# A two-block model's fp32 kernel: order of small stages in the mixer, and a shorter loop for overflowing experts

## The chip, the cores and the metric

One core of one Trainium2 chip runs the whole program in one launch. The metric is the device time of an execution in microseconds (us), the median over runs. PE stands for TensorE, DVE for VectorE, ACT for ScalarE, POOL for GpSimd, SP for SyncE.

## The reference

A sequence of 256 tokens of width 1024 passes two models' blocks, all in float32. The first block has a mixer (a gated delta rule with four heads in both directions over a context and the sequence, beside a Fourier mix) and a gated convolutional network. Norms are modulated by vectors made of a conditioning vector. The second block has two layers, each with a mixer, a layer of 32 experts of which each token uses two, and a gated embedding.

```python
mod_l = (silu_c @ w_ada[i] + b_ada[i])[:, None, :]                 # six rows of 1024: shifts, scales, gates
p = h @ w_in_l                                                     # u | q, k, v | z | a, b
qkv = silu(dwconv1d(p[..., o1:o2], conv_l)); q, k = l2norm(q), l2norm(k)
beta = sigmoid(ab[:, :, 0:2])
g = -exp(a_log) * softplus(ab[:, :, 2:4] + dt_bias)                # log decay
a_mat = where(strict, (kb @ kc.T) * decay, 0)                      # per chunk and head
t_inv = triangular_solve(eye + a_mat, eye)                         # then the scan over chunks
y_f = einsum(real(fft2(u)), w_f); y_d = rmsnorm(o) * silu(z)
y = concatenate([y_f, y_d]) @ w_out
...
h = h + hier_moe(rmsnorm(h), ...)                                  # silu(x @ w_gate[e]) * (x @ w_up[e]) @ w_down[e]
gate = sigmoid(rmsnorm(h) @ w_ple_gate + b); h = h + gate * (p @ w_ple)
```

## The kernel before

Activations stand transposed, features on the 128 partitions and tokens along the free axis. Each engine has a program written out by hand, in one order, and engines meet by counting semaphores. Dense weights come in chunks of 128 x 4096 floats (2 MB) into a ring of tiles in SBUF (`ring`), in the order of the table `DENSE`; SP issues the loads one after another (L420), each behind a wait for the products that used the slot's last content. `plan()` works these waits out.

Large projections use three rounded products in place of one fp32 product: ACT rounds a chunk half by half (`split_half`, L1232), and POOL (L1683) or DVE (`weights_low`, L1796) subtracts it from the chunk, which leaves the remainder. PE's `split_product` (L527) waits for the remainder of each half. All other products are fp32 (`dense`, L520), and PE carries out each fp32 product as two matmul instructions with two weight loads, and each transpose as one with one.

Results of `dense` and of the projections go through four PSUM banks in turn. `USES` numbers these uses in PE's order; use n takes bank n modulo 4, may start when use n - 4 is released, and counts up the semaphore `dense_full` when done. So `USES` is an order that PE, ACT, DVE and the load plan share.

The first block's mixer goes as follows. The projection w_in has five chunks: k and v (two), q, z, u. DVE does the short convolutions (L1900 to L1903), ACT the silu. The gates' logarithm is a chain of small DVE instructions (`log1p`, L1840 to L1848). For the l2 norms of six head tiles (four of k, two of q) DVE squares (L1934), PE sums over partitions (`sums_qk`, L671), ACT takes the root as a logarithm and an exponential (`root`, L1212 and L1213), DVE multiplies (L1950). In between ACT copies finished banks out (`to_sbuf`, L1325). After the Fourier weight products dft_w come the sums of the decay rates (L713) and, through `heads` (L704), the products of keys with keys and the rows of decay and beta; DVE takes differences (L1969), POOL masks (L1704), ACT exponentiates, DVE makes the key matrices (L1982), eight in number, counted by `at_ready`. DVE then inverts all 32 by 32 diagonal blocks in 31 steps of two instructions (L2020, L2022), with the column copies of the modulation (`ada_columns`, L2012) after steps 7, 12, 17 and 22, while PE transposes v and k (L696), and does the Fourier products (dft_b, dft_y) and parts 1 and 2 of the modulation. A part is four row products (L625, each with a chunk of its own), each followed by a copy of the row out of its bank, and four column products that turn the row into columns (through L520). Then the triangular solve goes on in larger blocks (L788 onward), which waits for DVE's solve and for all uses of part 2, and ACT copies diagonal blocks behind its last row copy.

The expert layers run in hardware loops over pairs of experts, four pairs to a turn on PE (L1084). Each expert has 64 slots; tokens beyond them go through an overflow loop over all experts under a branch on a flag (L1093 on PE, others on SP, ACT and DVE). Behind the branch PE starts the projection of the embedding's gate, whose first matmul (L527) needs the first of eight remainders that DVE makes (`weighted_low`, L1786); DVE multiplies the bank of that projection at L2340.

## Time and profile before

| what | value |
|---|---|
| median of 3 runs | 1750.52 us (1749.62 to 1752.70) |
| the profiled execution | 1751.42 us |
| its span, first to last instruction | 1749.6 us |
| mean granted TensorE clock | 0.973 |
| PE / DVE / ACT / POOL busy | 94% / 41% / 29% / 13% |
| moved by DMA | 528.27 MB, mean 302 GB/s |

The span is what all times in rows are counted from; the execution's own time is 1.8 us longer. A busy PE is not PE at its peak, since the ends of matmuls are modelled. The granted clock is a share of full speed (2.4 GHz); 0.50 is the lower level, 1.2 GHz. "issue" means that the engine waited for nothing that the profile shows.

### The profile page before, as it was taken

The page shows a single profiled execution, that of the slowest core. Times are in us where ns is not written, and L with a number is a line of the kernel's source. Part 1 is how long each engine was busy: PE and PEld are TensorE (multiplying, and loading weights), DVE is VectorE, ACT ScalarE, POOL GpSimd, SP SyncE. Part 2 cuts the span into 40 slices and gives each one's busy share as a digit, 9 for nine tenths or more (in the row PEclk, how much of TensorE's full clock was granted, in tenths as well). Part 3 has the DMA queues.
Part 4 walks back from the last instruction along what each step waited for, and adds up shares of the span by engine and source line. Part 5 has one row for each costly group of instructions (what it writes and reads, how often), then busy time and mean ns, then how long its engine had stood idle before and what let it go on. Part 6 is the DMA issues. An engine that isn't in the chain of part 4 may idle for free.

```text
span 1749.6 us, 25579 instructions
## 1 busy us (share of the span) xinstructions
PE 1642.2 (94%) x10590; PEld 1119.9 (64%) x10590; DVE 722.9 (41%) x1348; ACT 506.8 (29%) x778; POOL 231.7 (13%) x151
## 2 busy tenths in 40 slices
PE   5989898999999999999999997998999999999997
PEld 2778597899989964554435453988645454445446
DVE  2565724899346631222212124679322121212134
ACT  3344335544444221111111114476211110111125
POOL 0406313488420000000000000000000000000000
PEclk9999979999999999999999999999999999999998
DMA  9213516244454679999999999225899999999990
GB/s 403 106 38 129 241 60 242 105 184 148 166 193 186 272 309 420 428 427 429 428 429 428 428 427 406 103 92 217 369 420 428 427 430 427 429 428 428 426 396 25
DMA packets 37958, 528.27 MB, mean 302 GB/s; under 512 B 4208, under 2 KB 4336, under 8 KB 5104
## 3 DMA queue, kind: packets, MB, share of 16 engines
q1 hardware_dynamic: 37296, 525.22, 72.3%
q10 hardware_dynamic: 576, 1.78, 0.3%
q8 instruction: 68, 1.11, 0.2%
q14 instruction: 18, 0.15, 0.0%
HBM read 525.94 MB, written 1.05 MB: 301 GB/s over the span
## 4 chain that ended last, share of the span: by engine, by line
PE 69%; DMA 18%; DVE 8%; ACT 3%; issue 1%; POOL 1%; SPq 0%; DVEq 0%; ACTq 0%
PE bank L527 22%; PE bank L1050 18%; DMA ring<-in_w_up 10%; PE bank L1080 9%; PE bank L995 5%; DMA ring<-in_dense 4%; DMA work<-in_w_up 4%; PE bank L520 2%; DVE ring_rounded L1796 2%; PE bank L1016 1%; PE bank L1017 1%; ACT ring_rounded L1232 1%; PE bank L599 1%; PE bank L704 1%; PE bank L1065 1%
## 5 line engine op out<-in xcount | busy, mean ns | idle before, releaser
L527 PE MATMUL bank<-work_rounded,ring_rounded 128*128 128x256 f32 (+1 forms) x2192 | 358.2, 294 | 20.4 <-DVE xn_rounded L1786 7.1
L1050 PE MATMUL bank<-ring,work 128*64 128x512 f32 x1536 | 339.3, 596 | 17.7 <-DMA ring<-in_w_up 15.5
L527 PEld LDWEIGHTS bank<-work_rounded,ring_rounded 128*128 128x128 f32 x2192 | 310.3, 193 | 30.4 <-issue 16.3
L527 PE MATMUL bank<-xn_rounded,ring_rounded 128*128 128x256 f32 (+1 forms) x1536 | 276.3, 292 | 3.9 <-DVE xn_rounded L1780 3.4
L1050 PEld LDWEIGHTS bank<-ring,work 128*64 128x64 f32 x1536 | 114.1, 138 | 235.0 <-issue 221.9
L527 PEld LDWEIGHTS bank<-xn_rounded,ring_rounded 128*128 128x128 f32 x1536 | 224.5, 196 | 8.4 <-issue 4.4
L2286 DVE TENSOR_TENSOR work<-work,bank 128x512 f32<-128x512 f32 x32 | 22.0, 688 | 420.1 <-PE bank L1050 420.1
L1683 POOL TENSOR_TENSOR ring_rounded<-ring,ring_rounded 128x2048 fp32r<-128x2048 f32 (+1 forms) x37 | 159.5, 4329 | 209.9 <-ACT ring_rounded L1232 209.9
L1749 POOL TENSOR_TENSOR work<-work_rounded,work 128x128 f32<-128x128 f32 x64 | 24.2, 399 | 1139.3 <-PE bank L1073 825.8
L1080 PE MATMUL bank<-ring,work 128*64 128x512 f32 x768 | 170.1, 596 | 0.0
L1232 ACT ACTIVATE ring_rounded<-ring 128x2048 fp32r<-128x2048 f32 (+1 forms) x84 | 147.6, 1802 | 51.4 <-DMA ring<-in_dense 26.2
L995 PEld LDWEIGHTS bank<-work_rounded,work 128*128 128x128 f32 x1024 | 117.7, 193 | 24.7 <-issue 24.3
L1796 DVE TENSOR_TENSOR ring_rounded<-ring,ring_rounded 128x2048 fp32r<-128x2048 f32 (+1 forms) x47 | 102.4, 2203 | 58.3 <-ACT ring_rounded L1232 58.1
L995 PE MATMUL bank<-work_rounded,work 128*128 128x128 f32 x1024 | 123.2, 279 | 0.0
L2297 DVE SCALAR_TENSOR_TENSOR xn_rounded<-bank,work,work_rounded 128x512 fp32r<-128x512 f32 x64 | 48.0, 750 | 177.3 <-ACT work_rounded L1549 177.3
L1050 PE MATMUL bank<-work 128*64 128x512 f32 x512 | 112.8, 593 | 5.8 <-DMA work<-in_w_up 5.8
L1080 PEld LDWEIGHTS bank<-ring,work 128*64 128x64 f32 x768 | 53.0, 137 | 99.9 <-issue 99.9
L1539 ACT ACTIVATE work<-bank 128x512 f32<-128x512 f32 x30 | 18.0, 599 | 323.6 <-PE bank L995 323.6
L1549 ACT ACTIVATE work_rounded<-bank,work 128x512 fp32r<-128x512 f32 x64 | 44.0, 687 | 178.5 <-PE bank L1080 178.3
L2271 DVE TENSOR_TENSOR hT<-hT,bank 128x512 f32<-128x512 f32 x136 | 84.9, 682 | 8.9 <-PE bank L1017 8.9
L1050 PEld LDWEIGHTS bank<-work 128*64 128x64 f32 x512 | 38.1, 137 | 78.4 <-issue 78.4
L2104 DVE SCALAR_TENSOR_TENSOR work<-bank,params,work 128x189 f32<-128x189 f32 (+2 forms) x176 | 76.1, 432 | 6.2
(333 smaller groups left out, 1702.9 us busy)
## 6 DMA issues: line engine op xcount, KB each, us to landing
ring<-in_dense SPq DMA_DIRECT2D x48, 2048.0 KB, 7.9
ring<-in_w_gate SPq DMA_DIRECT2D x48, 2048.0 KB, 21.8
ring<-in_w_up SPq DMA_DIRECT2D x48, 2048.0 KB, 24.7
ring<-in_w_down SPq DMA_DIRECT2D x48, 2048.0 KB, 27.0
work<-in_w_gate SPq DMA_DIRECT2D x16, 2048.0 KB, 23.2
work<-in_w_up SPq DMA_DIRECT2D x16, 2048.0 KB, 25.6
work<-in_w_down SPq DMA_DIRECT2D x16, 2048.0 KB, 27.0
ring<-in_dense SPq DMA_DIRECT2D x8, 1408.0 KB, 6.2
```

Of the source, the lines that this page charges most:

```text
L520: last = mm(bank[n % BANKS][:, a:b], w, x, start=k == 0, stop=k == len(products) - 1)
L527: last = mm(out, rv(high_store[r][:, at:at + P]), rv(x[part][k]), start=opens and k == 0 and j == 0, stop=closes and k == n_k - 1 and j == 2)
L995: last = mm(out, xtok[:, u, k], rv(oneh[:, u].rearrange("p x s -> p (x s)")).bitcast(F32), start=u == 0, stop=u == NH - 1)
L1050: ins = mm(b[64 * y:64 * y + 64, :], xg[:, k, 64 * y:64 * y + 64], ws[y][:, 512 * k:512 * k + 512], start=k == 0, stop=k == KT - 1)
L1080: ins = mm(bank[6 + half][64 * y:64 * y + 64, :], hidT[:, j, 64 * y:64 * y + 64], ws[y][:, at:at + 512], start=j == 0, stop=j == 3)
L1232: signal(act.activation(rv(high_store[HIGH_SLOT[n]][:, a:b]), w[:, a:b], ACT.Copy), "w_high")
L1549: act.activation(rv(y_high[half]), bank[6 + half][:], ACT.Identity, scale=slot_w).then_inc(S["y_high"], 1)
L1683: pool.tensor_tensor(rv(w), w, rv(high_store[HIGH_SLOT[n]][:, a:b]), ALU.subtract).then_inc(S["w_low"], 1)
L1796: v.tensor_tensor(rv(w), w, rv(high_store[HIGH_SLOT[n]][:, a:b]), ALU.subtract).then_inc(S["w_low_dve"], 1)
L2104: ins = v.scalar_tensor_tensor(dst, x[:, r0 + dy:r1 + dy, c0 + dx:c1 + dx], par("w_dwc", 9 * f + 3 * (dy + 1) + dx + 1, 1), dst, ALU.mult, ...
L2271: v.tensor_tensor(hT[:, pair], hT[:, pair], bank[(5, 2, 3, 5)[q]][:].rearrange("p (k t) -> p k t", k=2), ALU.add)\
L2297: ins = v.scalar_tensor_tensor(rv(y_low[half]), bank[6 + half][:].rearrange("p (k t) -> p k t", k=2), slot_w, rv(y_high[half]).rearrange(" ...
```

## The change

It does five things. The overflow loop's body on PE becomes one for a half of the tokens, run 64 times, with wide products and transposes back in place of 32 narrow ones; DVE copies the half into a tile first, and copies the result out before the transposes. The remainders of chunk 3 of w_in (z) come ahead of the query convolutions on DVE, with ACT's rounding moved ahead too; chunk 4's (u) are put among the norms. On ACT the roots come ahead of the copies of z. On PE two groups of key products come ahead of the sums of the rates. And parts 1 and 2 of the modulation are spread: rows 0 and 1 of part 1 come between the token-major transposes and the Fourier products dft_b, row 0 of part 2 ahead of dft_y, with `USES` renumbered and a second buffer for rows (`ada_row`). Renamings through `ada_use` elsewhere are left out here.

```diff
@@ -85,10 +85,16 @@
 N_DENSE = sum(count for _, count, _ in DENSE)
 SPLIT = ("w_in", "w_out", "w_up", "w_down", "w_in_a", "w_out_a", "ple0", "w_in_b", "w_in_y", "w_out_b", "ple1")
-USES = [("ada0", 8), ("kv", 8), ("q", 2), ("z", 2), ("u", 2), ("dft_w", 2), ("vtok", 4), ("ktok", 4), ("dft_b", 4),
-        ("ada1", 8), ("dft_y", 2), ("ada2", 8),
+USES = [("ada0", 8), ("kv", 8), ("q", 2), ("z", 2), ("u", 2), ("dft_w", 2), ("vtok", 4), ("ktok", 4), ("ada1", 3), ("dft_b", 4),
+        ("ada1b", 5), ("ada2", 1), ("dft_y", 2), ("ada2b", 7),
         ("w_out", 4), ("up", FT), ("down", 4), ("in_a", 12), ("out_a", 4), ("ple0", 4), ("in_b", 4), ("gates0", 8), ("in_y0", 2), ("gates1", 8), ("in_y1", 2),
         ("out_b", 4), ("ple1", 4)]
+
+def ada_use(use, part, i):
+    first = (8, 3, 1)[part]
+    return use[f"ada{part}"] + i if i < first else use[f"ada{part}b"] + i - first
...
@@ -104,10 +110,10 @@
         use[name] = at
         at += count
     free = {}
-    for stage in ("ada0", "ada1", "ada2"):
+    for part in range(3):
         for c in range(4):
-            free[first[stage] + c] = ("dense_full", use[stage] + max(1, 2 * c))
+            free[first[f"ada{part}"] + c] = ("dense_full", ada_use(use, part, max(0, 2 * c - 1)) + 1)
     for c, last in enumerate((4, 8, 10, 12, 14)):
         free[first["w_in"] + c] = ("dense_full", use["kv"] + last)
...
@@ -309,7 +315,8 @@
     sqk = wk("cat", 1024).rearrange("p (n t) -> p n t", n=2)
     sqo = wk("kc", 1024).rearrange("p (n t) -> p n t", n=2)
     o_rstd = wk("kc", 1024, 1024).rearrange("p (n t) -> p n t", n=2)
-    ada_row = wk("cat", 1024, 1024).rearrange("p (m n) -> p m n", m=2)
+    ada_row = [wk("cat", 1024, at).rearrange("p (m n) -> p m n", m=2) for at in (1024, 0, 1024)]
     c_cols = wk("S", KT * 32).rearrange("p (k m) -> p k m", k=KT)
     ab_rows = wk("S", 512, 512)
...
@@ -704,14 +710,10 @@
                 last = mm(out[:, P * h:P * h + P], left(h), right(h), start=start, stop=stop)
             return last
-        for n in (USE["u"], USE["u"] + 1, USE["dft_w"], USE["dft_w"] + 1):
+        for n in (USE["u"], USE["u"] + 1):
             released(pe, n)
         pe.wait_ge(S["gates_ready"], 1)
         pe.wait_ge(S["qk_norm"], 6)
-        rates = glog.rearrange("p u c -> p (u c)")
-        for i, m in enumerate((cums[0], cums[1], ones)):
-            last = mm(bank[7][:, 32 * i:32 * i + 32], m, rates, start=True, stop=True)
-        signal(last, "gc_mm")
         def key_products(u, b):
...
@@ -734,8 +736,14 @@
             signal(heads(b, lambda h: beta[:, u, h:h + 1].to_broadcast([P, P]), lambda h: ident), "b_rows")
         key_products(0, 4)
+        key_products(1, 5)
+        for n in (USE["dft_w"], USE["dft_w"] + 1):
+            released(pe, n)
+        rates = glog.rearrange("p u c -> p (u c)")
+        for i, m in enumerate((cums[0], cums[1], ones)):
+            last = mm(bank[7][:, 32 * i:32 * i + 32], m, rates, start=True, stop=True)
+        signal(last, "gc_mm")
         decay_rows(0)
-        key_products(1, 5)
         for e in (1, 2, 3):
             decay_rows(e)
...
@@ -759,20 +767,23 @@
         token_major("vtok", vc)
         token_major("ktok", kc)
+        for m in range(2):
+            ada_step(1, m)
         for x in range(2):
             for u in range(NH):
                 dense(USE["dft_b"] + 2 * x + u, [
                     (P * g, P * g + P, [(uT[:, g, P * u:P * u + P], fo_w[:, x, P * g:P * g + P])]) for g in range(4)])
-        for m in range(5):
+        for m in range(2, 5):
             ada_step(1, m)
+        ada_step(2, 0)
         for b in range(4):
             released(pe, USE["dft_b"] + b)
         for b in range(2):
             dense(USE["dft_y"] + b, [
                 (SEQ * i, SEQ * i + SEQ, [(fo_b[:, x, u, 2 * b + i], fo(("cos_l", "sin_l")[x], SEQ * u, SEQ))
                                           for x in range(2) for u in range(NH)]) for i in range(2)])
-        for m in range(5):
+        for m in range(1, 5):
             ada_step(2, m)
...
@@ -781,6 +792,8 @@
         pe.wait_ge(S["solved"], 2)
         pe.wait_ge(S["att_ready"], 4)
+        for b in range(2):
+            released(pe, USE["dft_y"] + b)
         for s in range(2):
             for pair in range(2):
...
@@ -1091,27 +1104,31 @@
             over = pe.value_load(flag[0:1, 0:1], min_val=0, max_val=1)
             with pe.If(over > 0):
-                with pe.Fori(0, E) as e:
-                    pe.wait_ge(S[f"ov_full{layer}"], e * 48 + 48)
-                    for u in range(NH):
-
-                        pe.wait_ge(S[f"ov_add{layer}"], e * 2 + u + 1)
-                        for b in range(2):
-                            for k in range(KT):
-                                last = mm(bank[b][:], xnT[:, k, P * u:P * u + P], ring[2 * b + 1][:, 512 * k:512 * k + 512],
-                                          start=k == 0, stop=k == KT - 1)
-                        last.then_inc(S[f"ov_gu{layer}"], 1)
-                        pe.wait_ge(S[f"ov_hh{layer}"], e * 2 + u + 1)
+                with pe.Fori(0, NH * E) as n:
+                    pe.wait_ge(S[f"ov_add{layer}"], n * 2 + 1)
+                    for b in range(2):
+                        for k in range(KT):
+                            last = mm(bank[b][:], xg[:, k], ring[2 * b + 1][:, 512 * k:512 * k + 512],
+                                      start=k == 0, stop=k == KT - 1)
+                    last.then_inc(S[f"ov_gu{layer}"], 1)
+                    pe.wait_ge(S[f"ov_hh{layer}"], n * 2 + 1)
+                    for j in range(4):
+                        last = nc.tensor.transpose(bank[4][:, P * j:P * j + P], hh[:, P * j:P * j + P], ident)
+                    last.then_inc(S[f"ov_t{layer}"], 1)
+                    pe.wait_ge(S[f"ov_ht{layer}"], n + 1)
+                    for half in range(2):
                         for j in range(4):
-                            last = nc.tensor.transpose(bank[4][:, P * j:P * j + P], hh[:, P * j:P * j + P], ident)
-                        last.then_inc(S[f"ov_t{layer}"], 1)
-                        pe.wait_ge(S[f"ov_ht{layer}"], e * 2 + u + 1)
-                        for f in range(KT):
-                            out = bank[6 + f // 4][:, P * (f % 4):P * (f % 4) + P]
-                            for j in range(4):
-                                last = mm(out, ring[5][:, D * j + P * f:D * j + P * f + P], hidT[:, j],
-                                          start=j == 0, stop=j == 3)
-                        last.then_inc(S[f"ov_down{layer}"], 1)
+                            last = mm(bank[6 + half][:], hidT[:, j], ring[5][:, D * j + 512 * half:D * j + 512 * half + 512],
+                                      start=j == 0, stop=j == 3)
+                    last.then_inc(S[f"ov_down{layer}"], 1)
+                    pe.wait_ge(S[f"ov_hh{layer}"], n * 2 + 2)
+                    for half in range(2):
+                        for q in range(4):
+                            last = nc.tensor.transpose(bank[2 + half][:, P * q:P * q + P], y_high[half][:, P * q:P * q + P], ident)
+                    last.then_inc(S[f"ov_down{layer}"], 1)
                 pe.wait_ge(S["moe_done"], layer + 1)
                 nc.tensor.nop()
...
@@ -1303,12 +1320,16 @@
         functions(SILU)
         for i in range(8):
+            if i == 7:
+                split_next()
             released(act, USE["kv"] + i)
             x = (kc if i < 4 else vc)[:, i % 4]
             signal(act.activation(x, x, ACT.Silu), "silu_ready")
-            if i in (3, 7):
+            if i == 3:
                 split_next()
         for b in range(2):
+            if b:
+                split_next()
             released(act, USE["q"] + b)
             signal(act.activation(qc[:, 2 * b:2 * b + 2], qc[:, 2 * b:2 * b + 2], ACT.Silu), "silu_ready")
         act.wait_ge(S["ab_dve"], 1)
@@ -1317,7 +1338,6 @@
         functions(LN_EXP)
         act.wait_ge(S["ab_dve"], 2)
         signal(act.activation(gtmp[1], gtmp[1], ACT.Exp, scale=-1.0), "ab_act")
-        split_next()
         def to_sbuf(stage, b, out):
...
@@ -1325,14 +1345,14 @@
             free(act.activation(out, bank[(USE[stage] + b) % BANKS][:], ACT.Copy), USE[stage] + b)
         for a in range(6):
-            if a in (0, 1):
-                to_sbuf("z", a, wk("zs", 512, 512 * a))
             if a == 4:
                 to_sbuf("u", 0, wk("oT", 512))
             if a >= 2:
                 act.wait_ge(S["qk_norm"], a - 1)
             root(bank[4 + a % 2][:], bank[6 + a % 2][:], 1.0, "qk_ss", "qk_rstd")
+            if a in (0, 1):
+                to_sbuf("z", a, wk("zs", 512, 512 * a))
         to_sbuf("u", 1, wk("oT", 512, 512))
         for x in range(2):
...
@@ -1356,23 +1376,25 @@
         for stage, tile in (("vtok", "vtok"), ("ktok", "ktok")):
             for u in range(4):
                 to_sbuf(stage, u, wk(tile, 512, 512 * u))
+        def ada_rows(part, ms):
+            for m in ms:
+                n = ada_use(USE, part, max(0, 2 * m - 1))
+                full(n)
+                if m >= 2:
+                    full(ada_use(USE, part, 2 * m - 2))
+                free(act.activation(ada_row[part][:, m % 2], bank[n % BANKS][:], ACT.Copy), n)
+        ada_rows(1, (0, 1))
         for x in range(4):
             to_sbuf("dft_b", x, fo_b[:, x // 2, x % 2].rearrange("p g e -> p (g e)"))
-
-        def ada_rows(part):
-
-            for m in range(4):
-                n = USE[f"ada{part}"] + max(0, 2 * m - 1)
-                full(n)
-                if m >= 2:
-
-                    full(USE[f"ada{part}"] + 2 * m - 2)
-                free(act.activation(ada_row[:, m % 2], bank[n % BANKS][:], ACT.Copy), n)
-
-        ada_rows(1)
+        ada_rows(1, (2, 3))
+        ada_rows(2, (0,))
         for b in range(2):
             to_sbuf("dft_y", b, wk("cat", 512, 512 * b))
-        ada_rows(2)
+        ada_rows(2, (1, 2, 3))
         functions(SILU)
         signal(act.activation(wk("zs"), wk("zs"), ACT.Silu), "silu_ready")
...
@@ -1917,13 +1939,14 @@
                 dve.wait_ge(S["ab_dve"], 1)
                 after(v.tensor_tensor(gtmp[0], ab[:, :, 8:16], par("dt_bias").unsqueeze(1).to_broadcast([P, 4, 8]), ALU.add))
                 signal(v.scalar_tensor_tensor(gtmp[1], gtmp[0], -1.0, gtmp[0], ALU.mult, ALU.max), "ab_dve")
+        weights_low(FIRST["w_in"] + 3)
         for b in range(2):
             n = USE["q"] + b
             x = full(n)
             for i in range(2):
                 ins = conv3(n, qc[:, 2 * b + i], x[:, SEQ * i:SEQ * i + SEQ], conv_w(2 * b + i))
             free(ins, n)
-            weights_low(FIRST["w_in"] + 3, (b,))
         heads_of = [wk("kc", 512, 512 * h) for h in range(4)] + [wk("qc", 512, 512 * h) for h in range(2)]
...
@@ -1933,21 +1956,28 @@
                 dve.wait_ge(S["qk_ss"], a - 1)
             signal(v.tensor_tensor(sqk[:, a % 2], heads_of[a], heads_of[a], ALU.mult), "qk_sq")
+        def norm_qk(a):
+            dve.wait_ge(S["qk_rstd"], a + 1)
+            r = bank[6 + a % 2][:]
+            x = heads_of[a]
+            signal(v.scalar_tensor_tensor(x, x, 1.0 if a < 4 else float(P) ** -0.5, r, ALU.mult, ALU.mult), "qk_norm")
         square_qk(0)
         square_qk(1)
+        weights_low(FIRST["w_in"] + 4, (0,))
+        for a in range(2):
+            square_qk(a + 2)
+            norm_qk(a)
+        weights_low(FIRST["w_in"] + 4, (1,))
         dve.wait_ge(S["ab_act"], 3)
         log1p(gtmp[2], gtmp[1], gtmp[3:5])
         after(v.scalar_tensor_tensor(gtmp[0], gtmp[0], 0.0, gtmp[2], ALU.max, ALU.add))
         signal(v.scalar_tensor_tensor(glog, gtmp[0], -1.0, alog_e.unsqueeze(1).to_broadcast([P, 4, 8]), ALU.mult, ALU.mult),
                "gates_ready")
-        weights_low(FIRST["w_in"] + 4)
-        for a in range(6):
+        for a in range(2, 6):
             if a + 2 < 6:
                 square_qk(a + 2)
-            dve.wait_ge(S["qk_rstd"], a + 1)
-            r = bank[6 + a % 2][:]
-            x = heads_of[a]
-            signal(v.scalar_tensor_tensor(x, x, 1.0 if a < 4 else float(P) ** -0.5, r, ALU.mult, ALU.mult), "qk_norm")
+            norm_qk(a)
         shape = [P, HEADS, P]
```

## Rows read from the trace of the kernel before

**Rows 1.** The page, part 1: busy us, share of the span, instructions

```profile
PE 1642.2 (94%) x10590; PEld 1119.9 (64%) x10590; DVE 722.9 (41%) x1348; ACT 506.8 (29%) x778; POOL 231.7 (13%) x151
```

**Rows 2.** The chain of waits, 0 to 400 us: start us, us, what

```profile
111.28 7.27 PE bank L527 x36
...
127.91 1.10 PE bank L671 x2
129.00 5.70 PE bank L527 x48
```

**Rows 3.** Timeline of PE: start us, us, engine, line, tiles, count, idle before

```profile
111.28 0.58 PE L527 MATMUL bank<-work_rounded,ring_rounded 128*128 128x256 f32 x1 [3.82 <-DVE ring_rounded L1796]
...
148.21 8.20 PE L704 MATMUL bank<-consts,work 128*128 128x128 f32 x72
```

**Rows 4.** Timeline of DVE, 94 to 205 us

```profile
94.12 0.75 DVE L1900 TENSOR_SCALAR work<-bank,params 128x512 f32<-128x512 f32 x1 [3.25 <-PE bank L527]
...
96.83 0.19 DVE L1919 SCALAR_TENSOR_TENSOR work<-work 128x32 f32<-128x32 f32 x1
...
103.23 2.28 DVE L1796 TENSOR_TENSOR ring_rounded<-ring,ring_rounded 128x2048 fp32r<-128x2048 f32 x1
...
149.30 0.69 DVE L1969 TENSOR_TENSOR xn<-bank,work 128x512 f32<-128x512 f32 x1 [1.03 <-PE bank L704]
...
164.38 1.13 DVE L1982 SCALAR_TENSOR_TENSOR xn<-bank,work,xn 128x128 f32<-128x128 f32 x4 [0.77 <-ACT xn L1354]
...
181.99 0.17 DVE L2012 TENSOR_TENSOR mod<-bank,params 128x8 f32<-128x8 f32 x1
...
204.93 0.24 DVE L2012 TENSOR_TENSOR mod<-bank,params 128x8 f32<-128x8 f32 x2
```

**Rows 5.** Timeline of ACT around 97 us

```profile
97.01 3.70 ACT L1232 ACTIVATE ring_rounded<-ring 128x2048 fp32r<-128x2048 f32 x2
```

**Rows 6.** The chain of waits, 176 to 208 us

```profile
176.23 7.60 DMA ring<-in_dense
...
185.81 8.89 PE bank L520 x48
194.70 1.90 PE bank L625 x16
...
205.19 2.74 PE bank L625 x16
```

**Rows 7.** Busy us (instructions) of each engine by window, granted clock, DMA share, GB/s

```profile
111.20:117.20 6.00, 5.92 (x27) 5.92 (x28) 5.15 (x19) 5.14 (x5) 0.00 (x0) 0.50 0.01 3
...
181.90:183.80 1.90, 0.02 (x1) 0.00 (x0) 1.73 (x7) 0.00 (x0) 0.00 (x0) 1.00 0.99 423
...
217.00:240.00 23.00, 22.12 (x286) 21.90 (x285) 5.16 (x10) 5.28 (x12) 5.23 (x6) 0.50 0.12 39
```

**Rows 8.** Timelines of PE and DVE after the expert stages

```profile
1092.18 0.55 PE L527 MATMUL bank<-work_rounded,ring_rounded 128*128 128x256 f32 x1 [6.59 <-issue]
...
1104.97 0.69 DVE L2340 TENSOR_TENSOR work<-bank,work 128x512 f32<-128x512 f32 x1 [8.43 <-PE bank L527]
...
1708.06 3.25 DVE L1786 SCALAR_TENSOR_TENSOR xn_rounded<-hT,params,work_rounded 128x256 fp32r<-128x256 f32 x8
```

**Rows 9.** The chain of waits after the expert stages

```profile
1087.28 3.21 DVE xn_rounded L1786 x8
...
1092.18 8.11 PE bank L527 x48
...
1710.36 7.93 PE bank L527 x48
```

**Rows 10.** Windows as in rows 7: straight code, and the expert loop

```profile
740.00:990.00 250.00, 242.28 (x1330) 117.67 (x1328) 53.74 (x97) 31.54 (x63) 6.16 (x17) 1.00 1.01 428
...
1116.95:1135.24 18.29, 16.86 (x130) 16.25 (x129) 12.92 (x29) 10.50 (x16) 0.00 (x0) 1.00 0.31 116
```

**Rows 11.** DMA queues, 1705 to 1712 us, the only one: packets, MB, share

```profile
q8 instruction: 2, 0.03, 1.7%
```

More of the change, by code:

```diff
@@ L629, in ada_columns @@
         def ada_columns(part, m):
-            first = USE[f"ada{part}"]
-            released(pe, first + max(0, 2 * m - 1))
-            dense(first + min(2 * m + 2, 7), [
-                (P * i, P * i + P, [(ada_row[:, m % 2, P * i:P * i + P], con("sel"))]) for i in range(4)])
+            released(pe, ada_use(USE, part, max(0, 2 * m - 1)))
+            dense(ada_use(USE, part, min(2 * m + 2, 7)), [
+                (P * i, P * i + P, [(ada_row[part][:, m % 2, P * i:P * i + P], con("sel"))]) for i in range(4)])
         def ada_step(part, m):
@@ L791, in _ @@
         for n in (4, 5, 6, 7):
-            released(pe, USE["ada2"] + n)
+            released(pe, ada_use(USE, 2, n))
         for s in range(2):
@@ L2007, in ada_columns @@
         def ada_columns(part, m):
-            n = USE[f"ada{part}"] + min(2 * m, 7)
+            n = ada_use(USE, part, min(2 * m, 7))
             x = full(n)[:].rearrange("p (i c) -> p i c", i=4)[:, :, 0:2]
@@ L2317, in moe @@
                             .then_inc(S[f"ov_hh{layer}"], 1)
[L2318 to L2319 removed]
+                        dve.wait_ge(S[f"ov_down{layer}"], e * 4 + (u * 2 + 2))
+                        for b in range(2):
+                            last = v.tensor_copy(y_high[b], bank[6 + b][:])
+                        last.then_inc(S[f"ov_hh{layer}"], 1)
+                        dve.wait_ge(S[f"ov_down{layer}"], e * 4 + (u * 2 + 3))
                         for b in range(2):
                             x = hT[:, 4 * b:4 * b + 4, P * u:P * u + P]
[L2322 removed]
+                            last = v.tensor_tensor(x, x, bank[2 + b][:].rearrange("p (k t) -> p k t", k=4), ALU.add)
                         last.then_inc(S[f"ov_add{layer}"], 1)
[L2324 removed]
+                dve.wait_ge(S[f"ov_add{layer}"], 4 * E)
                 v.memset(rt(608, 1), 0.0)
```

19 lines of the change are left out of this document (8 added, 11 removed).

## The prediction

> **What bounds the kernel now.** I read the busy shares and the chain of waits first, then the waits on TensorE, then each engine's timeline where the change works. TensorE (PE) is busy 94% of the span [rows 1], so time can only come out of its pauses, of stretches at its lower clock, and of what follows them. Up to 330 us, and between and after the two expert stages, the loads on the SP queue wait for PE's progress and not the other way round; what shortens PE's path there should move everything behind it by as much. In the chain of waits the projection runs 48 matmuls in 5.70 us, but 36 in 7.27 us after a pause [rows 2]. The pause is 3.82 us, for VectorE's (DVE's) remainder of the gate weights z [rows 3]; behind it the granted clock was 0.50, the 1.2 GHz level [rows 7].
>
> **Part 1, gate remainders and roots.** DVE took the two remainders behind the query convolutions (2.28 us each, the first at 103.23) [rows 4]. Now they follow the gates' small work, which ended at 97.02 [rows 4]. They need ScalarE's (ACT's) rounded halves. That was 3.70 us of work at 97.01 [rows 5]; now it stands ahead of the last silu, and needs the kv products, whose end released DVE at 94.12 [rows 4]. So the halves exist at 95.9 and 97.8, and the remainders at 99.3 and 101.5. Query convolution 0 then runs 101.5 to 104.4, convolution 1 keeps its place. The last v silu slips by 1.3 us, and nobody reads it before the token products. z starts at 106.0 (12 matmuls before the pause) and has both remainders: the pause of 3.82 goes, and 36 matmuls cost 36 x 5.70 / 48 = 4.28 instead of 7.27, which is 2.99. At 127.91 PE had also waited 1.09 us for a root that stood behind a copy [rows 2]; with roots ahead of copies it is ready at 116.0, before the sums at 119.3. The remainders of the Fourier weights u end at 112.5 and 118.9 and are wanted at 121.0 and 122.4; the logarithm of the gates ends at 122.4 and the last norm at 130.8, against a use at 135.9. All are covered, the u halves by 3.5 us at least. Sum: 3.82 + 2.99 + 1.09 = **7.9 us** up to the end of the Fourier weight products.
>
> **Part 2, key products ahead of rates.** Two groups of key products (0.91 us each: 72 rows, nine groups, took 8.20) [rows 3] fill PE's wait for the last copy, and only then come the rates. The first decay difference moves by 8.1 us, the second, at 149.30 before [rows 4], by 8.95, since no key group lies before it any more. GpSimd's masks (its queue gets no new work) and the exponentials follow it, so the last key matrix, which ended at 165.51 [rows 4], ends at 156.5: **9.0 us** so far.
>
> **Part 3, modulation rows spread.** Before, PE reached the end of its last row product, R, at 205.19 + 2.74 = 207.93 [rows 6], held by transfers: a load issued after a row product landed 7.60 us later [rows 6]. DVE's solve was done by 204.93 [rows 4], so the path was PE's and the loads'. Now rows 0 and 1 of the second part come ahead of the Fourier products, and their slots are reloaded earlier: the four loads issued at about 164, 166, 176 and 179 land by 171, 176, 184 and 189, the last at 194, each ahead of its use (the tightest by 1.7 us). The DMA pauses go. A new wait comes: the banks are taken in turn, four in number, so the fourth Fourier product (use 38) needs what the first column product (use 34) left, and DVE frees that inside its solve after step 7, which stood at 181.99, 16.65 us after the last key matrix [rows 4]. So PE waits from about 169.2 to 173.2 and all that is queued on PE waits with it; ACT stands for the same product, with only copies behind it. From 173.2 the sum is one Fourier product 0.93, five column products 4.55 (0.91 each: 16 matmuls and dft_y were 8.89), six row products of 1.90 and dft_y 7.07 [rows 6]: 23.95 us, so R = 197.2. Later frees inside the solve (steps 12, 17, 22) come 3 to 9 us before PE needs them, and the one after the solve by 1 us. R would move by 10.7 us at the full clock. But the nearest pause, 3.8 us, was followed by 6 us at 0.50, while 1.9 us was followed by none [rows 3, 7]. I charge the dearer: 3.0 us, the cost worked out in part 1. **Part 3 ends at 7.7 us** over all three; the bounds are 7.7 and 10.7. What follows (triangular solve, state) hangs on R and moves with it.
>
> **Part 4, the overflow loop.** No row lies on its lines: no expert overflows, and its own speed is worth nothing. But PE jumps over it in both layers. The last scatter ended at 1085.6; PE's next matmul came at 1092.18, 6.59 us later, with "issue" as reason [rows 8]; in the second layer it came at 1710.36 [rows 9]. What it needs first is one of DVE's eight remainders, 0.41 us each, from 1087.22 and 1708.06 [rows 8, 9]: it could have started at 1087.8 and 1708.6. In the second stall only instruction packets were on the DMA engines, two of them [rows 11]. So I read it as the target's code coming from memory. Straight code needed one packet for 259 instructions, and in 250 us of the expert loop PE ran 2658 instructions [rows 10] without one packet, which speaks for jumps to loaded code being cheap. The loop's body was 2 x (48 fp32 products at four instructions and four transposes at two) = 400 instructions; it becomes 24 products and 12 transposes, 120 instructions: half a packet's code instead of one and a half. The rows do not show what a jump of 120 costs, so both ends stand: nothing gained, or all of it. I take all, since the target then lies in the packet at hand or the next one, which straight code has already asked for.
>
> The Trainium skill (Runtime: NRT & Kernel Launch, section Instruction fetch mechanics) says that prefetch is sequential in 16 KiB blocks and that a taken branch stalls if its target is not in the two-block window. By that rule the long jump is outside and the short one inside; without the rule this part could be anything between 0 and 10.8, with it it is the whole term.
>
> First layer: start 4.4 us earlier, and 48 matmuls took 8.11 [rows 9] where 5.70 is the full clock's price, 2.4 more: 6.8, or 4.4 if the clock still falls. DVE waited 8.43 us for the product behind it [rows 8], so it passes on: sums at 1095.3, gate product at 1098.2, with ACT's root at 1096.6 in time. Second layer: 1.75 earlier plus 7.93 - 5.70 = 2.2 [rows 9]: 4.0, or 1.75. There PE runs without a pause to the tail. The remaining pauses are 2.2 and 1.8 us, nearest to the 1.9 us with no fall [rows 7], so I take 6.8 + 4.0 = **10.8**. The new loop's other engines cost nothing.
>
> **Sum.** 7.7 + 10.8 = 18.5 us. The profiled execution took 1751.42 with a span of 1749.6, 0.9 above the median of 1750.52; against itself it would come to 1732.9, against the median to 1732.0. Bounds of this case: 7.7 + 4.4 + 1.75 = 13.9 (1736.6) and 10.7 + 10.8 = 21.5 (1729.0). The expert stages between are bound by the transfers' volume and start when PE frees slots, so they shift and absorb nothing.
>
> **Rivals.**
> - *The jump still stalls* (any taken jump out of a block asks for code again, or something else holds PE): only the mixer's 7.7 to 10.7 remain, 1742.8 to 1739.8. For it: no row shows a short jump over code. Against: the packets inside the stall, and the loop. Chance 0.10.
> - *The mixer gives nothing*, since the clock stays at 1.2 GHz from the new wait on, as it did from 217 to 240 [rows 7]: six rows at +0.84, columns and dft_y near double, some 12 us, eat the 10.7 and 1.6 more. Result 1750.5 + 1.6 - 10.8 = 1741.3. Against: falls behind single pauses ended after 6 us. Chance 0.07.
> - *Slower*: the first layer's skipped code is 280 instructions shorter, so the second layer's expert loop (2658 instructions in nearly three turns) lies differently against the 256-instruction packets, and may span one packet more than PE holds. Then each of its three turns ends in a jump like the one measured, 6.6 us and 2.4 of low clock, 27 us, hidden only so far as the loads are later. Result 1732 + 27 = 1759. It decides from 6.2 us per turn (past 18.5). Against: in the present alignment not one packet is fetched in the loop. Chance 0.02.
> - *No change*, jump and mixer both failing: 0.02.
>
> **Numbers.** Forecast case 0.79, 1732.0, own range 1729.0 to 1736.6. To leave out no more than 2 in 10 the range takes in the two rivals of 0.10 and 0.07 in most part, and a clock stretch at either end: 1727.5 to 1742.5. This kernel's measurement tells 0.2%, 3.5 us, from no change. Faster by more 0.95, within 0.03, slower 0.02.
>
> **What would show it.** z's matmuls without a pause near 106 at 2.4 GHz; the rates about 137.7; the last key matrix ending near 156.5; a PE pause of some 4 us before the fourth Fourier product, ended by DVE's column copy; the last row product of the mixer at 197 to 200, with no DMA wait in the rows; PE after each scatter pausing about 2 us, released by DVE's remainder, with no instruction packet in the pause. An "issue" pause over 3 us there, or a pause of PE in the second expert loop, would prove part 4 wrong; a last row product after 201, part 3.

## The result, and the profile after

The changed kernel takes **1738.03 us** (median of 4 runs, 1733.57 to 1740.67) against 1750.07: ratio 0.9927, with a 95% interval of 0.9903 to 0.9950. That is 12.0 us faster where 18.5 were forecast. The time lies inside the stated range of 1727.5 to 1742.5, 6 us above the number, and outside the forecast case's own range of 1729.0 to 1736.6; the interval reaches from 8.8 to 17.0 us, so 18.5 is excluded by it. The profiled execution took 1740.67 us, its span is 1738.9. The page, part 1, beside [rows 1]:

```profile
PE 1646.4 (95%) x10590; PEld 1120.6 (64%) x10590; DVE 722.8 (42%) x1348; ACT 506.9 (29%) x778; POOL 231.8 (13%) x151
```

PE's count of executed instructions has not changed, so all of the difference lies in pauses and in the clock.

**The mixer.** The chain of waits of the changed kernel, 93 to 206 us (start us, us, what), beside [rows 2, 6]:

```profile
93.14 0.35 PE bank L667 x4
93.49 17.31 PE bank L534 x144
110.80 1.72 PE bank L677 x4
112.52 5.65 PE bank L534 x48
...
136.45 0.59 PE bank L744 x6
...
154.04 1.13 DVE xn L2012 x4
...
171.89 0.18 DVE mod L2042
172.11 2.08 PE bank L527 x8
...
197.79 1.90 PE bank L632 x16
```

The 144 matmuls hold the gate product, at the full clock and without a pause. This execution reached the mixer 0.94 us earlier by chance (the four small products of L667 at its head began at 93.07, those of the kernel before, L661, at 94.01), so I count from there: the last key matrix ends at 62.1 us, before at 71.5. **9.4 us** gained, 9.0 forecast. The last row product ends at 106.6, before at 113.9: **7.3** gained, 7.7 forecast. Between them stands the new pause, in PE's and DVE's timelines:

```profile
172.11 2.08 PE L527 MATMUL bank<-work 128*128 128x128 f32 x8 [2.95 <-DVE mod L2042]
...
171.89 0.17 DVE L2042 TENSOR_TENSOR mod<-bank,params 128x8 f32<-128x8 f32 x1
```

Busy time of PE, PEld, DVE, ACT and POOL by window, then granted clock, DMA share and GB/s:

```profile
112.60:118.10 5.50, 5.50 (x49) 5.50 (x48) 4.00 (x4) 2.68 (x5) 0.00 (x0) 1.00 0.00 0
155.30:161.70 6.40, 6.40 (x32) 6.29 (x32) 6.37 (x4) 3.86 (x7) 4.42 (x5) 0.54 0.00 0
172.20:179.00 6.80, 6.80 (x32) 3.52 (x32) 3.62 (x10) 1.19 (x2) 0.95 (x1) 0.55 0.59 219
1081.00:1087.00 6.00, 6.00 (x31) 6.00 (x32) 5.55 (x8) 6.00 (x8) 0.00 (x0) 0.57 0.51 214
1698.50:1703.90 5.40, 5.40 (x26) 5.40 (x26) 4.70 (x9) 5.40 (x8) 0.00 (x0) 0.50 0.01 3
```

Around 115, where it had been at 0.50 [rows 7], the clock is full now. Behind the new pause it is at the lower level, as charged. The last two windows are the ones the forecast had at the full clock.

**The restarts behind the expert stages.** Timelines of PE and DVE, beside [rows 8]:

```profile
1080.91 0.55 PE L534 MATMUL bank<-work_rounded,ring_rounded 128*128 128x256 f32 x1 [2.44 <-DVE xn_rounded L1808]
...
1080.09 3.26 DVE L1808 SCALAR_TENSOR_TENSOR xn_rounded<-hT,params,work_rounded 128x256 fp32r<-128x256 f32 x8
...
1698.43 0.55 PE L534 MATMUL bank<-work_rounded,ring_rounded 128*128 128x256 f32 x1 [2.02 <-DVE xn_rounded L1808]
```

and the chain of waits, beside [rows 9]:

```profile
1080.91 8.28 PE bank L534 x48
...
1698.43 8.40 PE bank L534 x48
```

The pauses are 2.44 and 2.02 us, not 6.59 and 3.59, and DVE's remainder releases PE, as forecast. The trace records PE's jump instruction itself with 0.36 and 0.22 us, where it took 6.19 and 3.37. But the 48 matmuls did not get faster: 8.28 and 8.40 us. Before they took 8.11 and 7.93, and 5.70 is the price at the full clock.

### The profile page after: what moved, and what is told of

Read it like the earlier page. It is cut to its first block, busy times and chain, and to the rows that moved or that the text cites. A ratio compares the mean times of both kernels' runs of the same rounds, so it can differ in the third digit from the quotient of the medians.

```text
span 1738.9 us, 25580 instructions
## 1 busy us (share of the span) xinstructions
PE 1646.4 (95%) x10590; PEld 1120.6 (64%) x10590; DVE 722.8 (42%) x1348; ACT 506.9 (29%) x778; POOL 231.8 (13%) x151
## 4 chain that ended last, share of the span: by engine, by line
PE 69%; DMA 17%; DVE 8%; ACT 3%; issue 1%; POOL 1%; SPq 0%; DVEq 0%; ACTq 0%; POOLq 0%
PE bank L534 22%; PE bank L1063 18%; DMA ring<-in_w_up 10%; PE bank L1093 9%; PE bank L1008 5%; DMA work<-in_w_up 4%; DMA ring<-in_dense 3%; PE bank L527 2%; DVE ring_rounded L1818 2%; PE bank L1029 1%; PE bank L1030 1%; ACT ring_rounded L1249 1%; PE bank L606 1%; PE bank L632 1%; PE bank L710 1%
## 5 line engine op out<-in xcount | busy, mean ns | idle before, releaser
L534 PEld LDWEIGHTS bank<-work_rounded,ring_rounded 128*128 128x128 f32 x2192 | 307.8, 192 | 20.7 <-issue 10.6
```

Source lines behind the costliest of these rows:

```text
L534: last = mm(out, rv(high_store[r][:, at:at + P]), rv(x[part][k]), start=opens and k == 0 and j == 0, stop=closes and k == n_k - 1 and j == 2)
```

## The experiments

Two theories to begin with. **Theory**: the mixer gives some 7.6 us, and the restarts give only their earlier start, since the clock falls after a pause of 2 us just as after one of 6. **Rival**: the clock's 4.6 us were gained and something else, in the mixer's new pause or in the expert stages, took them.

### The parts alone

`e1_short_loop` is the kernel before with the new overflow block on all engines, `e2_mixer_only` the changed kernel with the old one, so its edit is the reverse. The head of the block on PE, for e1:

```diff
-                with pe.Fori(0, E) as e:
+                with pe.Fori(0, NH * E) as n:
...
```

> The kernel before with the short overflow loop alone (the change's parts on SP, PE and DVE for that loop). If the jump over the loop cost the fetch of code, PE's pauses behind the two expert stages fall from 6.6 and 3.6 us to about 2.4 and 2.0, DVE's remainder ends them, and the time falls by 4.1 + 1.6 = 5.7 us to about 1744.5 with the clock still low behind them, by up to 10.8 if it stays at 2.4 GHz. Rival: the jump is not what cost, and the changed kernel's shorter pauses come from elsewhere: pauses of 6.6 and 3.6 us and 1750 us.

> The changed kernel with the old overflow loop. If the parts add up, the mixer's share is left: its last row product ends near 200 us, the two pauses are 6.6 and 3.6 us again, and the time is 7 to 8 us under the kernel before, about 1743. Rival: the mixer gave nearly all of the 12 us measured, 1738; or nearly nothing (what it gains in its stage is lost later), 1750.

Measured: e1 1747.33 us (0.9982, 0.9972 to 0.9991), e2 1742.64 us (0.9957, 0.9942 to 0.9972), against 1750.21. So the mixer is worth 7.6 us (interval 4.9 to 10.1), where 7.7 were forecast. The short loop is worth 2.9 alone, less than the 5.7 expected for a clock that still falls. Beside the mixer's change it is worth 4.7 (1742.64 to 1737.90, the time of the changed kernel measured once more below; the kernels before that each was compared with differ by 0.7). The chains of e1 and then of e2 behind the expert stages:

```profile
1088.69 8.22 PE bank L527 x48
...
1705.74 8.55 PE bank L527 x48
```

```profile
1083.08 8.11 PE bank L534 x48
...
1701.62 7.82 PE bank L534 x48
```

Short pause or long, the price is the same. e1's jumps took 0.36 and 0.22 us, e2's 6.45 and 3.56.

### What makes the jump dear

`e3_pad140` and `e10_pad280` leave the short loop as it is and put products that never run into the block that is jumped over, so that the jump goes over 260 and over 400 instructions (e10 has 70 in place of 35):

```diff
+                for _ in range(35):
+                    mm(bank[0][:, 0:P], ident, ident, start=True, stop=True)
                 pe.wait_ge(S["moe_done"], layer + 1)
```

> The changed kernel with 35 fp32 products (140 instructions) more inside the branch behind the overflow loop; like the loop they are not run. In the changed kernel's first layer PE had run 248 instructions since the last packet of code when it met the branch, and landed near 391; now it lands near 531, beyond two packets of 256. In the second layer it had run 61, plus the shift of 140, and lands near 476. If what counts is whether the target lies within the packet at hand or the next, the first layer's pause is back (4 to 7 us, reason issue) and the second's is not (2 us). Rival: the length of the jump counts: both pauses grow alike, or neither. Rival: any change of length inside the branch is free.

> The changed kernel with 70 fp32 products added to the overflow block, ahead of its wait; none of them runs. The jump then goes over 400 instructions, as it did before the change, but the loop itself is the short one. Theory (the distance of the jump sets the stall, not what the skipped loop does): the jump instruction takes 6 us in the first layer and 3.5 us in the second, as in the kernel before, where it took 6.19 and 3.37; PE restarts 8 us and 5 us after the scatter; time near 1743. Rival (the loop's form, its semaphores or its registers, made the stall): 0.36 and 0.22 us, 1738.

e10: 1745.44 us in its one run, and the jump took 5.99 and 3.57 us. Its restarts in PE's timeline:

```profile
1085.56 0.55 PE L534 MATMUL bank<-work_rounded,ring_rounded 128*128 128x256 f32 x1 [6.39 <-issue]
...
1703.49 0.55 PE L534 MATMUL bank<-work_rounded,ring_rounded 128*128 128x256 f32 x1 [3.79 <-DVE xn_rounded L1810]
```

In the second line the profile names DVE, but DVE's remainders had begun at 1700.99, and the jump ended at 1703.22; it is the jump that held PE. With 280 instructions that never run the two stalls of the kernel before are back to within 0.2 us, so the length of the code that is jumped over makes them and not what the loop does. In both stalls one instruction packet of 0.02 MB is on the same DMA queue (q8) as in the kernel before. e3, at 260 instructions, took 1749.44 us in its one run and lies between:

```profile
1081.92 0.55 PE L534 MATMUL bank<-work_rounded,ring_rounded 128*128 128x256 f32 x1 [2.36 <-DVE xn_rounded L1810]
...
1085.92 0.79 PE L534 MATMUL bank<-work_rounded,ring_rounded 128*128 128x256 f32 x2 [1.95 <-issue]
...
1707.72 0.58 PE L534 MATMUL bank<-work_rounded,ring_rounded 128*128 128x256 f32 x1 [3.70 <-DVE xn_rounded L1810]
```

Its jumps took 0.36 and 0.35 us, and yet PE stood still in both layers. In the first it stopped for 1.95 us after the first matmuls behind the target, with "issue" as reason. In the second its pause was 1.7 us longer than after 120 instructions; the profile names DVE again, but PE's last wait had passed at 1705.92, and its first matmul came at 1707.72. So the expectation was missed: it had a pause of 4 to 7 us in the first layer and none in the second, from where the target lies among the packets of code. Neither that count nor a price by length alone, which was the rival, fits word for word; what happens between 120 and 400 instructions stays open. Not all that this one run lost lies there: at 1681 it waited 3.40 us for a load, where the changed kernel waits 1.87, and the clock fell there. I don't lay that to the jump.

### The clock behind the restarts

`e4_filler` gives PE something to do in the pause: four fp32 products nobody reads, between scatter and projection, in both layers.

```diff
+            for _ in range(4):
+                mm(bank[7][:], ones, consts[:, 0:512], start=True, stop=True)
```

> The changed kernel with four fp32 products of 512 columns (about 1.7 us, results unused) on PE between the branch and the first product of the embedding's gate, in both layers. If the clock falls there because PE stands still for 2 us, it now stays at 2.4 GHz, the 48 matmuls behind take 5.7 us in place of 8.3 and 8.4, and the time is about 4.6 us under the changed kernel, near 1733.5. Rival: the fall comes from the thin work before the branch (pauses and narrow products in the last scatter), the 48 matmuls still take 8.3 us, and the time is that of the changed kernel, 1738, or 1 us over.

It took 1737.04 us (0.9926, 0.9910 to 0.9943), 0.9 us below the changed kernel's 1737.90, which is within the noise, where 4.6 were expected. Its chain of waits:

```profile
1078.81 5.40 PE bank L1136 x8
1084.20 5.65 PE bank L534 x48
...
1694.98 3.70 PE bank L1136 x8
1698.68 5.65 PE bank L534 x48
```

The 48 matmuls run at the full clock in both layers. In the second the filler took 3.70 us, and the clock stayed at 1.00 through it and behind it. In the first the clock fell all the same, as its windows show:

```profile
1080.30:1083.60 3.30, 3.30 (x6) 1.39 (x5) 3.30 (x9) 3.30 (x7) 0.00 (x0) 0.67 0.89 370
1084.20:1089.80 5.60, 5.60 (x50) 5.60 (x49) 4.57 (x3) 4.10 (x3) 0.00 (x0) 1.00 0.08 32
```

The low stretch lies under the filler, which took 5.40 us in place of 3.70: it cost 1.7 us there, where it costs the 48 matmuls 2.6 in the changed kernel (8.28 - 5.70). So in the first layer the filler bore the low clock and did not prevent it, and what made it fall there (the thin work ahead of the branch, as the rival had it, or the 0.54 us that PE still paused) is open. The filler also holds PE past DVE's remainder: in the first layer PE starts 3.3 us later than it did at 1080.91. Four products were expected to take 1.7 us; they take 3.70 at the full clock.

### The spread and its new pause

`e5_early_column` moves the column copy that PE waits for from behind step 7 of DVE's solve to behind step 1. `e8_no_spread` puts the modulation rows back in one block, with the old `USES` and without the second row buffer. `e7_late_remainders` undoes the gate remainders alone: DVE makes them behind each query convolution again, and ACT rounds its second half behind the last silu. The core of each, in this order:

```diff
-            if j in (6, 11, 16, 21):
-                ada_columns(1, (6, 11, 16, 21).index(j) + 1)
+            if j in (0, 11, 16, 21):
+                ada_columns(1, (0, 11, 16, 21).index(j) + 1)
```

```diff
-        ada_rows(1, (0, 1))
...
-        ada_rows(1, (2, 3))
-        ada_rows(2, (0,))
+        ada_rows(1, (0, 1, 2, 3))
...
-        ada_rows(2, (1, 2, 3))
+        ada_rows(2, (0, 1, 2, 3))
```

```diff
-        weights_low(FIRST["w_in"] + 3)
...
+            weights_low(FIRST["w_in"] + 3, (b,))
```

> The changed kernel once more, as the yardstick of the others of this call. Both theories: 1738.0 us, between 1736.5 and 1739.5; the clock falls again behind both restarts after the expert stages (48 matmuls in 8.3 us), in every profile.

> The changed kernel with one edit: DVE copies the first column product of the second modulation part after step 1 of its solve, not after step 7. Theory (the new pause of 2.95 us ahead of the fourth Fourier product is this copy's alone, and the 6.8 us at the low clock behind it belong to the pause): no pause at 169, full clock from there, the last row product ends near 193.1 instead of 199.7, 6.6 us earlier. But DVE's solve with its two transposes ends at 198.1 whatever PE does, so the triangular solve starts at 198.2 instead of 201.55: 3.3 us off the time, about 1734.7 against 1738.0. Rival (the low clock comes from something else, such as the pause at 152 to 155): the pause goes, the low clock stays, the last row product ends near 196.7 and the solve starts at 198.6: nearly the same time, 1735.0, so the granted clock at 172 to 179 tells them apart. Second rival (another slot or a load is late next, since PE now comes 6 us earlier to the copies after steps 12, 17 and 22 and to the reloads): a DMA or DVE wait in the rows and no gain, 1738.

> The changed kernel with the modulation rows put back in one block behind the Fourier products, all else kept. Theory (the spread itself loses 2.1 us: from the last key matrix to the last row product the changed kernel takes 44.5 us where the kernel before took 42.4): the last row product ends near 197.6 instead of 199.7, the pause on DVE's column copy is gone, DMA waits in the rows are back; time 2.1 us below the changed kernel, 1736.0. Rival (the spread pays, as the loads were the limit before): the loads hold the rows, the last row product ends at 201 or later and the time is 1739.5 or more.

> The changed kernel with the gate remainders put back behind the query convolutions (and ScalarE's second half behind its last silu); the roots stay ahead of the copies. Theory (the remainders are worth the pause of 3.8 us and the clock of 3.0 us behind it): pause and low clock are back in the gate product, the last key matrix ends 6.8 us later, and the time is 6.8 us above the changed kernel, 1744.8. Rival (the pause's place is taken by slack further on, at the Fourier weights and the norms): less than 4 us of it reach the last key matrix, 1742 or less.

All against a kernel before of 1749.53 us:

| kernel | us | ratio, 95% interval | key matrices done | solve on PE starts |
|---|---|---|---|---|
| changed, once more | 1737.90 | 0.9940 (0.9926 to 0.9954) | 62.1 | 107.0 |
| e5_early_column | 1732.98 | 0.9909 (0.9893 to 0.9925) | 62.1 | 103.8 |
| e8_no_spread | 1739.11 | 0.9943 (0.9930 to 0.9956) | 62.1 | 106.7 |
| e7_late_remainders | 1745.20 | 0.9975 (0.9963 to 0.9987) | 68.8 | 112.3 |

(The last two columns are us from the start of the same early products, L661 or L667; the kernel before has 71.5 and 116.6, the first profile of the changed kernel 62.1 and 108.5.)

**e7** costs 7.3 us, where 6.8 were expected. The pause is back as it was, in its timeline of PE:

```profile
110.90 0.58 PE L534 MATMUL bank<-work_rounded,ring_rounded 128*128 128x256 f32 x1 [3.82 <-DVE ring_rounded L1816]
```

and so is the low clock, in its windows:

```profile
111.00:117.00 6.00, 6.00 (x30) 6.00 (x31) 3.26 (x3) 2.03 (x4) 0.00 (x0) 0.53 0.01 3
```

The key matrices come 6.7 us later, and 3.82 + 2.99 of part 1 is 6.8. The 2.7 us that are left to 9.4 I lay to the roots and the order of the key products (1.09 + 1.1 by the forecast); no run takes these two apart.

**e5** gains 4.9 us, where 3.3 were expected. There is no pause at 169, and the windows of its trace show the full clock behind it, which the theory wanted and the rival did not:

```profile
168.90:176.00 7.10, 6.95 (x58) 3.66 (x56) 6.49 (x19) 1.79 (x3) 0.95 (x1) 1.00 0.99 420
```

What I had missed is that DVE's solve gets faster too: in the changed kernel DVE had stood 3.08 us in its solve for a column product that PE's pause had delayed. This wait goes, and the solve's last transposes start 3.3 us earlier, counted from the early products (190.36 - 92.40 against 194.31 - 93.07). They are on the path that ends last now: the last column product waits for a copy that DVE makes behind them, and the triangular solve starts when it is done.

```profile
194.27 2.02 PE L527 MATMUL bank<-consts,work 128*128 128x128 f32 x16 [1.45 <-DVE mod L2042]
```

**e8** was expected at 1736.0, or at 1739.5 or more by the rival. It came out at 1739.11, 1.2 us above the changed kernel and within the noise of it, and its solve starts at 106.7 where that of the changed kernel starts at 107.0 and 108.5. Its waits for loads are back, in its timeline of PE:

```profile
175.24 2.52 PE L631 MATMUL bank<-ring,work 128*32 128x512 f32 x16 [2.44 <-DMA ring<-in_dense]
...
197.29 1.92 PE L631 MATMUL bank<-ring,work 128*32 128x512 f32 x16 [2.02 <-DMA ring<-in_dense]
```

So the spread by itself is worth nothing that can be measured here: its new pause costs what the waits for loads cost. The 2.1 us that the expectation laid to it came from one profile. The second profile of the changed kernel has the new pause at 4.13 us, but less low clock around it, and starts the solve 1.5 us earlier.

**The changed kernel once more** repeats the time. The expectation that the clock falls equally in every profile was wrong:

```profile
1080.96 7.47 PE bank L534 x48
...
1697.84 5.95 PE bank L534 x48
```

Six profiles without added work have the short pauses (the changed one twice, e1, e5, e7, e8). In the first layer the 48 matmuls took 7.47 to 8.69 us, 8.3 in the mean; in the second 5.95 to 8.66, 7.9 in the mean. With pauses of 3.6 to 6.9 us (before, e2, e10) they took 7.8 to 8.1. After the same 2.0 us pause the clock mostly falls, and once it did not.

### Both edits together

`e6_both` is e5 and e4 in one; `e9_small_filler` has two extra products in place of four:

```diff
-            for _ in range(4):
+            for _ in range(2):
                 mm(bank[7][:], ones, consts[:, 0:512], start=True, stop=True)
```

> The changed kernel with the early column copy and with four extra 512-wide fp32 products (their result is not read) between the last scatter and the projection, in both layers. Theory (the two edits act on different places, and each is worth what it was alone, 4.9 and 0.9 us): 1732.1 us. Rival (the copy's gain is what the chain can take, since the solve's transposes end it): 1733 or more.

> As e6_both, but two extra products in place of four: 1.85 us at the full clock, less than the pause of 2.0 us, where four took 3.70 us and held PE for 1.7 us beyond DVE's remainder. Theory (the clock falls for PE's idleness, so filling most of the pause keeps it, and now nothing is delayed): 48 matmuls in 5.7 us behind the second restart, starting 1.9 us after the jump; about 1.3 us less than e6_both, 1730.8. Rival (a pause of 0.2 to 0.6 us plus the one at the scatter's hand-over is still enough for the clock to fall): 8 us for the 48 matmuls and 1733, as the early column alone.

e6: **1730.47 us** (0.9892, 0.9875 to 0.9908), against 1749.78. e9: 1731.00 us (0.9890, 0.9873 to 0.9906). Chains of waits of e6, then of e9:

```profile
1070.68 5.40 PE bank L1136 x8
1076.07 5.70 PE bank L534 x48
...
1687.68 3.70 PE bank L1136 x8
1691.38 5.71 PE bank L534 x48
```

```profile
1077.54 5.88 PE bank L534 x48
...
1693.16 5.68 PE bank L534 x48
```

In the second layer two products are followed by the full clock as four are. In the first neither kept it: under the fillers the granted clock was 0.61 in e6 (1070.68 to 1073) and 0.58 in e9 (1074 to 1077). From the start of PE's jump to the end of the 48 matmuls, the six kernels with a short pause and no filler took 10.6 and 10.0 us in the mean (first and second layer), e4 11.5 and 9.6, e6 11.5 and 9.7, e9 9.7 and 7.9. By the traces, then, four products gain nothing and two gain 2.8 us. The times don't show this difference: e6 was expected at 1732.1 and e9 1.3 us below e6, and they lie within 0.5 us of each other. Over e5 the fillers are worth 2.5 and 2.0 us, four products over the changed kernel 0.9, and all these intervals overlap, so no time here proves a gain by the filler. Both kernels beat the kernel before and the changed one, and the early column copy alone does so too.

## Why the prediction was right, and where it was off

- **Parts 1 and 2, right.** The key matrices end 9.4 us earlier (9.0). e7 confirms 6.7 of it as the pause and its clock; the rest is not taken apart.
- **Part 3, right in place and size.** The new pause stands where forecast, ended by DVE's column copy: 2.95 and 4.13 us in two profiles (about 4 forecast), with the low clock behind it (charged). No row waits for a load. The last row product gained 7.3 us in the first profile and 8.8 in the second (200.00 against a start at 94.92), forecast 7.7. In the first profile the clock was also low ahead of the new pause (0.54 at 155.3 to 161.7), which was not in the sum. e2 puts all three parts at 7.6 us of time.
- **Part 4, the stall right.** It was the jump over the long block. It goes, and DVE's remainder releases PE in both layers: 4.15 and 1.57 us earlier (6.59 - 2.44, 3.59 - 2.02), forecast 4.4 and 1.75. One detail of its rows was misread: of the two instruction packets of [rows 11] one lies inside the second stall (one packet from 1706.8 to 1710.2). The Trainium skill (Runtime: NRT & Kernel Launch, section Instruction fetch mechanics) says that a taken branch stalls if its target is outside a window of two blocks. For the jump over the block the trace agrees with the prediction's reading of it: 6.19 and 3.37 us over 400 instructions, 0.36 and 0.22 over 120. For the expert loop it does not: each turn of it holds 1200 or more matmuls and weight loads, and its jumps took 0.08 to 0.24 us.
- **The step that failed** is the term of the clock in part 4: "The remaining pauses are 2.2 and 1.8 us, nearest to the 1.9 us with no fall [rows 7], so I take 6.8 + 4.0". The 4.6 us in it were not gained. The 48 matmuls took 0.2 us more in the first layer and the same in the second (means of six profiles against 8.11 and 7.93). I had one row of a pause with no fall and let it stand for a rule. Matmuls at the full clock behind a short pause do occur, 5.95 us once in twelve, and 5.65 to 5.88 behind a filler.
- **A term that was missing.** Behind the last DVE instruction the kernel before needs 3.3 us to its end (1749.6 - 1746.34), the changed one 4.2 (1738.9 - 1734.72). It is 3.3 in e2, the only other kernel with the old overflow block, and 4.2 in all the kernels with the new one, so it comes with that block. In the last 5 us of the changed kernel the DMA queues are:

```profile
q1 hardware_dynamic: 288, 1.05, 10.0%
q14 instruction: 1, 0.01, 0.1%
```

In e1 and e10 the same packet of instructions lies among the two output stores; before and in e2 there is none, and the stores land 2.8 us after their issue in place of 3.2 to 3.7. That the packet causes the 0.9 us is not shown, since no run has the one without the other.
- **Luck.** Even the lower bound of the forecast case, 13.9 us (1736.6), had the clock falling behind both restarts, and the measured 12.0 lie below it, mostly by the 0.9 us at the output stores and the 0.4 that the restarts gave less. The time fell inside the stated range because that had been widened to 1742.5 for two rivals that did not come up.

The account, in us:

| term | forecast | measured |
|---|---|---|
| mixer | 7.7 | 7.6 (e2) |
| earlier restarts | 6.15 | 5.7 |
| clock behind them | 4.6 | -0.2 |
| output stores | 0 | -0.9 |
| sum | 18.5 | 12.2 |

The sum agrees with the 12.0 measured, more closely than its parts are known (4.9 to 10.1 for the mixer alone). The three terms below the mixer are read from profiles, each of one execution. For e1 the same terms, with its own 48 matmuls (8.22 and 8.55, 0.7 more than before), give 4.1, where 2.9 was measured with an interval of 1.6 to 4.9. Of the rivals, the stalling jump is excluded by the short pauses in all kernels with the short block, and the silent mixer by e2; the slower case did not come up, since no turn of the second expert loop stalls (its three jump instructions took 0.08 to 0.23 us in the changed kernel).

## What to carry to other kernels

A pause that gets shorter need not give back the clock behind it: here pauses of 2.0 to 2.4 us were followed by as much low clock as pauses of 3.6 to 6.9. So charge the low clock for a pause that remains, as one bound, and put work into it only as long as the pause is: by the traces, four products that nobody reads held PE back longer than they gained in the first layer. When a product is moved up in a shared order of banks, look for the release that it now waits for, and put that release just as early: here one copy, moved by six steps, gave 4.9 us, and the wait it caused on DVE was part of the price. Code that is never run can cost time where an engine jumps over it (here 6.2 and 3.4 us over 400 instructions, 0.4 and 0.2 over 120), so keep rare blocks short.

## What was not expected of the hardware

- A taken jump took 0.2 to 0.4 us over 120 instructions, the same over 260 but with a standstill of 1.95 and 1.8 us at or shortly behind the target (one run), and 3.4 to 6.5 over 400 (before, e2, e10). At the same 400 the first layer pays 6.0 to 6.5 and the second 3.4 to 3.6 in each of the three. Loads of weights fill the DMA engines during the first stall (82.9% in e10) and none runs during the second; that this is the reason was not tried.
- The same pause of 2.0 us was followed by the low clock in most profiles and by the full one in one of them, so one profile does not price a clock term. Work put into the pause was followed by the full clock in the second layer of three kernels, and in the first layer of the same three the clock fell during that work.
- One packet of instructions among the last stores, with 0.9 us more to the end, in all eleven profiles with the new block and in neither of the two with the old one.
